# Three moves on TensorE in a three-layer kernel: the bias table's products to the start, two identity products out, two value products ahead of their levels

## The reference

```python
bias = t5[t5_bucket(offs), g].T
logits = jnp.einsum('bqhd,bqjhd->bqhj', qb, kgat).astype(jnp.float32) * scale + bias32[None, None]
...
top_val, top_idx = lax.top_k(fine_sel, TOP_K)
```

## Time and profile before

| | |
|---|---|
| time, median of three runs | 1578.17 us (1578.12 to 1578.44) |
| the profiled execution's own time | 1578.25 us |
| its span, first to last instruction | 1575.5 us |
| TensorE busy | 1450.5 us, 92% |
| VectorE busy | 790.1 us, 50% |
| ScalarE busy | 317.4 us, 20% |
| HBM read | 377.25 MB |
| mean granted TensorE clock | 0.959 of 2.4 GHz |

### The profile page before, as it was taken

One profiled execution on the slowest core, in us unless ns is written; L12 is line 12 of the kernel. 1 busy time (PEld: TensorE's weight loads), 2 busy tenths in 40 slices (PEclk: granted clock), 3 DMA queues, 4 the chain that ended last, 5 costly groups with the idle time before them and its releaser, 6 DMA issues.

```text
span 1575.5 us, 20364 instructions
## 1 busy us (share of the span) xinstructions
PE 1450.5 (92%) x8450; PEld 1017.4 (65%) x8450; DVE 790.1 (50%) x1533; ACT 317.4 (20%) x668; POOL 22.7 (1%) x41
## 2 busy tenths in 40 slices
PE   9999999999999999999999999999999577576577
PEld 6798898999445998898998446655544233133132
DVE  4888567756666977658656656534321000001001
ACT  3235430122002226330221002334400000000000
POOL 0000000000000000000000003100000000000000
PEclk9999999999999999999999999999999788788789
DMA  9574334444453534344444456555899999999998
GB/s 337 179 266 161 108 108 160 161 161 162 190 183 101 187 112 157 108 161 161 161 161 161 179 191 204 182 212 197 315 384 426 426 427 427 426 427 427 427 418 315
DMA packets 114925, 380.23 MB, mean 241 GB/s; under 512 B 10836, under 2 KB 23252, under 8 KB 104144
## 3 DMA queue, kind: packets, MB, share of 16 engines
q1 hardware_dynamic: 111952, 369.53, 61.3%
q0 software_dynamic: 2880, 9.36, 1.9%
HBM read 377.25 MB, written 5.73 MB: 243 GB/s over the span
## 4 chain that ended last, share of the span: by engine, by line
PE 79%; DMA 18%; SPq 2%; DVE 1%; issue 0%; ACT 0%; DVEq 0%
DMA ring<-in_w 17%; PE bank L1553 13%; PE bank L1606 12%; PE bank L1379 9%; PE bank L1187 7%; PE bank L1194 6%; PE bank L1303 4%; PE bank L1756 4%; PE bank L1351 3%; PE bank L1327 2%; PE bank L1655 2%; PE bank L1526 1%; PE bank L1528 1%; PE bank L1252 1%; PE bank L1278 1%; SPq L971 1%
## 5 line engine op out<-in xcount | busy, mean ns | idle before, releaser
L1756 PE MATMUL bank<-ring,region 128*32 128x512 f32 x208 | 113.9, 711 | 50.7 <-DMA region<-in_w 50.7
L1756 PE MATMUL bank<-region 128*32 128x512 f32 x512 | 114.1, 709 | 44.8 <-DMA ring<-in_w 44.8
L1606 PE MATMUL bank<-region 128*128 128x512 f32 x320 | 140.6, 592 | 0.0
L1187 PE MATMUL bank<-hT,ring 128*128 128x256 f32 x512 | 115.2, 381 | 0.0
L1606 PEld LDWEIGHTS bank<-region 128*128 128x128 f32 x320 | 60.5, 190 | 74.6 <-issue 74.6
L1187 PEld LDWEIGHTS bank<-hT,ring 128*128 128x128 f32 x512 | 95.5, 190 | 13.6 <-issue 1.0
L1553 PE MATMUL bank<-region 128*128 128x128 f32 x768 | 100.5, 275 | 0.0
L1553 PEld LDWEIGHTS bank<-region 128*128 128x128 f32 x768 | 93.0, 192 | 0.0
L1756 PEld LDWEIGHTS bank<-region 128*32 128x32 f32 x512 | 28.8, 129 | 89.3 <-issue 89.3
L1756 PEld LDWEIGHTS bank<-ring,region 128*32 128x32 f32 x208 | 25.5, 129 | 83.9 <-issue 83.9
L1817 PE MATMUL bank<-region 128*32 128x512 f32 x192 | 60.8, 735 | 17.5 <-DMA hT<-in_w 15.7
(11 more groups left out here) (500 smaller groups left out, 2666.8 us busy)
## 6 DMA issues: line engine op xcount, KB each, us to landing
region<-in_w SPq DMA_DIRECT2D x43, 2048.0 KB, 38.7
ring<-in_w SPq DMA_DIRECT2D x30, 2048.0 KB, 37.8
ring<-in_w_in SPq DMA_DIRECT2D x26, 2048.0 KB, 8.7
ring<-in_w_up SPq DMA_DIRECT2D x16, 2048.0 KB, 8.1
ring<-in_w_down SPq DMA_DIRECT2D x32, 1024.0 KB, 6.3
own_slot<-in_w SPq DMA_DIRECT2D x7, 2048.0 KB, 43.2
ring<-in_w_out SPq DMA_DIRECT2D x6, 2048.0 KB, 7.7
region<-in_w SPq DMA_DIRECT2D x22, 512.0 KB, 8.6
```

The lines of the kernel that those rows point to most:

```text
L1187: t = mm(b[:, 0:T], w[:, k, :], act[:, k, :], start=(k == 0), stop=(k == KD - 1))
L1606: t = mm(b[:, :], left[:, t2, :], right[:, t2, :], start=(c4 == 0 and t2 == 0), stop=(c4 == 7 and t2 == 1))
L1756: t = mm(b[32 * e:32 * e + 32, :], xg[:, k, 32 * e:32 * e + 32], four[e][c][:, 512 * (k % 2):512 * (k % 2) + 512], start=(k == 0), stop=(k ...
```

## The change

Four places, all of order or count:

- The table's three products go from behind the memory turns to behind the first turns of x, in the place of the two idle products of 512 columns. VectorE's part goes to its first norm, behind its first eviction. GpSimd no longer waits for x's second half before it loads the table. The three banks are given out earlier in the same way.
- `spin(7, 3)` becomes `spin(7, 1)`.
- At levels 4 and 6 of each mixer the last attention step of the level, `("dp", 1)` and `("dp", 2)`, moves ahead of the level's own products.

```diff
--- before.py
+++ after.py
@@ -232,11 +232,12 @@
     for j in range(LEVELS):
         n = 3 if j < 4 else 2
         s.append(("lm", j))
-        s += att[at:at + n - 1]
+        early = n if j in (4, 6) else n - 1
+        s += att[at:at + early]
         s += [("hx",)] if j == 0 else [("hl", j, 0)] if j < LEVELS - 1 else [("hl", j, 0), ("hl", j, 1)]
         if j + 2 < LEVELS:
             s.append(("lv", j + 2))
-        s += att[at + n - 1:at + n]
+        s += att[at + early:at + n]
         at += n
         s += g(2 if j < 2 else 1)
 
@@ -623,6 +624,8 @@
         for l in range(DEPTH):
             if l == 0:
                 give_turns(l, "hT", 0)
+                for g in range(DIL_G):
+                    bk.give((2, "t5", g))
             bk.give((l, "d", 0))
             give_turns(l, "hT", 1)
             bk.give((l, "d", 1))
@@ -633,8 +636,6 @@
                 if n == "kv":
                     give_turns(2, "memT", 0)
                     give_turns(2, "memT", 1)
-                    for g in range(DIL_G):
-                        bk.give((2, "t5", g))
                 if n in ("iq", "hi", "si"):
                     fam = "hh" if n == "hi" else n
                     for m in GATE_ORDER:
@@ -1100,7 +1101,6 @@
 
         @block.gpsimd
         def _(pool):
-            pool.wait_ge(x_late_loaded, 16)
             pool.dma_start(t5_onehot, a["c_t5"]).then_inc(t5_loaded, 16)
             pool.dma_start(t5_rows, a["c_t5m"]).then_inc(t5_loaded, 16)
             pool.dma_start(t5_tab, a["t5_table_2"]).then_inc(t5_loaded, 16)
@@ -1391,7 +1391,7 @@
             for l in range(DEPTH):
                 if l == 0:
                     turn_half(0, 0)
-                    idle_products(2, 512)
+                    distance_rows()
                 first_rows(N_MIX[l], [(l, "d", i) for i in range(NT)], arrived((l, "d")) if l else slot(0), raw_tile)
                 for name, cols, _ in projections(l)[1:-4]:
                     if name == "hi":
@@ -1405,7 +1405,6 @@
                     if name == "kv":
                         turn_half(N_MEM, 0)
                         turn_half(N_MEM, 1)
-                        distance_rows()
                         memory_rows(arrived((0, "kv"))[:, :, 0:cols])
                         continue
                     if name != "hg":
@@ -1675,7 +1674,7 @@
                 token_major((2, "router", i), wr, h_tile, i, (1,))
 
             before, ones = sbmask[:, 0:P], sbmask[:, P:2 * P]
-            spin(7, 3)
+            spin(7, 1)
             pe.wait_ge(picks_made, 1)
             b, chosen = bank_of((2, "rank")), fine[4]
             mm(b[:, 0:32], before, chosen[:, 0, :], start=True, stop=True)
@@ -2230,8 +2229,8 @@
                     if j in ACT_TURNS[n] or n in N_MLP and j == 1:
                         continue
                     turned_rows(n, j)
-                if n == N_MEM:
-                    distance_rows()
+                    if (n, j) == (0, 1):
+                        distance_rows()
                 dve.wait_ge(ss_ready, n + 1)
                 if n in N_MLP:
                     link(V.tensor_scalar(sd[:, n, :], ss[:, n, :], 1.0 / D, EPS, ALU.mult, ALU.add))
```

## The result

The change made the kernel slightly slower where the prediction had it faster by 2.15 us: the median of 22 executions is 1579.74 us against 1578.09 us of before, ratio 1.0013, 95% interval 1.0007 to 1.0019. (The ratios are those on record and not quotients of the medians; that would be 1.0010 here.) The range (1574.0 to 1578.7) does not hold it. The profiled execution took 1578.34 us with a span of 1576.6 us, 1.1 us longer than the span of before.

A forecast was written before the change was run, and what follows sets the result against it. TensorE was taken to bound the kernel up to 1143 us, then DMA a fixed-length expert stage from 1147 us. Terms -1.5 - 0.9 + 0.25 = -2.15 us gave 1576.0 us; range 1574.0 to 1578.7.

The forecast's parts named there:

- Part 1: Table products moved to the start: 0.94 us added there, 2.45 us saved at the memory rows, -1.5 us in all.
- Step (b): At the start: the table's 217.5 KB delay x's first half by 0.5 us, covered because the turns start later anyway.
- Step (c): At the start: the first weights, delayed, are there by 9.9 us, before TensorE asks for them at 10.3 us.
- Rival 3: Clock falls behind the table products; the dense projection loses 1.7 us, -0.45 us in all, 1577.7 us; chance 0.08.
- Step (a): At the start: the table, issued at 1.6 to 1.9 us, lands without a stall; other end 0.4 us.
- Rival 4: Table lands late at the start: nothing gained from 7.9 us after its third issue, 1581.4 us at worst; chance 0.05.
- Part 2: Value products ahead of levels 4 and 6 fill TensorE's 0.44 us wait at level 4: -0.9 us in two layers.
- Part 3: One identity product instead of three at the choice of experts: +0.25 us, ends -1.48 and +1.2 by the clock.
- the return of the clock: At the choice of experts: full clock back between 1144.6 and 1147.2 us, middle 1145.9, within the first expert products.
- The lower end: At the choice of experts: the ranking starts at 1139.98 instead of 1141.46 us, -1.48 us if nothing else changes.
- The term around the span: Outside the profiled span: 2.75 us of the execution's 1578.25 us, kept in the forecast time.
- The measure: At the expert stage: the end moves as much as the first free expert weight slot, at 1146.73 us before.

The follow-up runs named there:

- early_loads: The kernel before with one edit: GpSimd loads the table without waiting for x's second half, all products where they stood; ratio 1.0010.
- start_only: The kernel before with only the bias table's loads and products moved to the start, as in the change; ratio 1.0018.
- no_identity_cut: The change with three identity products kept: table's loads on GpSimd and products at the start, value products ahead; ratio 1.0002 against the kernel before.
- levels_only: The kernel before with only the two value products moved ahead of levels 4 and 6; ratio 0.9991.
- mended_change: The whole change, but with SP loading the table behind x's first half and GpSimd none of it; ratio 0.9992 against the kernel before.
- sp_table_levels: The change with three identity products kept and SP loading the table behind x's first half; 1573.39 us, ratio 0.9976 against the kernel before.

## Why the prediction was wrong

**Part 1** was forecast at -1.5 us and lost 2.0 in the profile. Three of its steps failed:

- *Step (b)*, "x's first half ... 0.5 us ... covered": the table's bytes were divided by the full DMA rate. Here x came 2.0 us late (6.2 instead of 4.2 us), and the turns started at 7.52 and not at 5.93 us; 0.65 us came back since they took 1.06 and not 1.71. In three other profiles with the same loads x was 0.2 to 1.2 us late, so 2.0 is the worst case seen. Step (c) would have failed next: where x was hardly late (`early_loads`), TensorE waited 1.8 us for the weights.
- *Rival 3*, at 0.08, was real, and the largest of the three: the clock falls behind the table products. It was priced at 1.7 us; the eight dense products took 5.40 instead of 3.60 us, 1.8. That in the old place the clock stayed at 1.00 had been held against it; in two later profiles it fell there as well.
- *Step (a)*, no stall for the table: TensorE stalled 0.5 us for it in the profile even behind a late x, and 1.4 us in `start_only` and `no_identity_cut`. The table landed at 2.43 + 6.6 = 9.03 us; the forecast had its issue at 1.6 to 1.9. Rival 4 named this mechanism with 7.9 us as its point, which was not reached.

The two other terms were right: +0.94 us for the longer products, and at the memory rows the way from the dense products of the second half to them, which start at 13.50 us before and 17.88 after, got shorter by (40.45 - 13.50) - (42.47 - 17.88) = 2.4 us (forecast 2.45).

**Part 2**: the mechanism is shown, the size was half. The 0.44 us per layer was the wait; `levels_only` gave 0.92. The move at level 6 was counted as what keeps the gain. By the rows it was not needed for that: VectorE's last preparation itself moved from 201.14 to 200.63 us in that run and ended at 201.85, where the value products of level 6 start at 201.88. It earns some 0.2 us by order alone. No run moved level 4 without level 6. (The list of TensorE's waits before has one larger entry than the 0.9 us of L2799, 1.5 us ahead of its first idle products, which no part touches.)

**Part 3**: forecast +0.25 with +1.2 as the end for the clock. SP's issue came 1.41 us later where all work ahead of the router was 0.2 us late: +1.2 us, the end itself. The step that failed is the return of the clock at "1145.9", a middle of two rows from another stage; it returned behind the first expert products, which took 3.64 us. The lower end, -1.48, did not exist: it came from an execution whose identity products were slow. And that the upper end was met is luck. The gather lost 0.92 us and not a half of 1.13: the 1.71 us of the earlier trace rows was no price of the lower clock, as the granted share reads 1.00 in that stretch and the same turns took 1.04 to 1.90 us in other profiles. The ranking, counted with it, ran at full clock. `mended_change`, against executions with identity products at full clock, lost 13.00 - 10.05 = 2.95 us, beyond both ends.

**The term around the span** was taken as 2.75 us and was 1.74 in the profile. With 2.75 us there, the time would have missed the forecast by 1.0 us more.

**The measure**, the first free expert slot, held in all: from SP's issue to the end of the span 428.4 to 428.7 us in both kernels of the change, in `levels_only` 1572.2 - 1143.73 = 428.5 and in `sp_table_levels` 1571.5 - 1142.67 = 428.8.

## What to carry to other kernels

A load placed ahead of critical bytes must be priced by its shape as well as its size: the one here, on 32 and 4 partitions, delayed the bytes behind it more than twice as much as the same bytes on 128 partitions did. Useful products in the place of idle ones must be looked at for their width: thin ones fill the time and may lose the clock. Compare the spans as well as the times. And before a gain is read from one profile, look whether the clock in that stretch was low by chance of that execution.

## What the runs showed of the hardware

The kernel before has two times: of its 22 executions 9 took 1576.1 to 1576.8 us and 13 took 1577.9 to 1578.9. The profiles show two places where the clock makes such a difference; which of them made which execution they do not say, as only one execution of this kernel has a profile. One is the memory's projection behind the table products (14.00 or 15.70 us, above). The other is the choice of experts. From the start of the router's last sixteen products to SP's issue the way took 10.05 or 10.06 us in eight profiles with three identity products (`levels_only`: 1143.73 - 1133.68) and 11.46 to 11.48 in five others, the kernel before among them (1146.80 - 1135.33 = 11.47), where the identity products ran at 1.2 GHz; in `start_only` the low clock came behind them (11.56). With one identity product it was 11.35, 12.68 and 13.00 us: never as short as 10.05. So the three dense products do not prevent the low clock, but in thirteen of fourteen profiles the clock was high from the gather on.
